# 24 selection steps moved from the prompt to the latent stage, and the prompt's scores in four single banks three heads ahead of their turns

## The chip, the cores and the metric

One core of one Trainium2 chip runs the whole program. The metric is the device time of one execution in microseconds (us); lower is better. Five engines appear: PE (TensorE, the matmul array), DVE (VectorE), ACT (ScalarE), POOL (GpSimd) and SP (SyncE, which issues DMAs). PE reads from SBUF and writes into PSUM, eight banks of 512 f32 columns on each of 128 partitions.

## The reference

The program is one step of a decoder trunk of two layers, on 528 prompt tokens (16 learned ones and 512 given) and on 64 new sample tokens (8 sequences of 8, each with 2048 cached positions). Each layer is a half feed-forward block, an attention block with two groups of eight heads, and another half feed-forward block, each with a layer norm. The two head groups:

```python
# latent heads ("M" in the kernel)
s = (einsum('bqhr,bkr->bhqk', q_lat, c_kv) + einsum('bqhd,bkd->bhqk', q_pe, k_pe)) * scale
p = softmax(where(key_pos <= q_pos, s, -inf)); o_lat = einsum('bhqk,bkr->bqhr', p, c_kv)
# sparse heads ("D"): an indexer picks, for each query, the top_k keys that all 8 heads use
score = einsum('bqh,bqhk->bqk', w_idx, relu(einsum('bqhd,bkd->bqhk', q_idx, k_idx)))
_, sel = lax.top_k(where(key_pos <= q_pos, score, -inf), top_k)   # 132 for prompt, 256 for samples
s = q . k[sel] * 64**-0.5;  o = softmax(s) @ v[sel]
```

The choice of keys is exact: it goes by the order of f32 scores. For the prompt it is needed per query tile, for the samples once per layer, before their sparse heads.

## The kernel before, in words

A loop of two turns (one per layer) runs the stages feed-forward, projection, sample index scores, prompt attention, latent attention of the samples, sparse attention of the samples, output projection, feed-forward, with a barrier between stages. Two stages are touched, and one helper.

**Selection steps.** The 256 best of each sample query's index scores are found in 32 rounds: MAX8 (line L1264) finds the eight best of a row of 1032 values, and MATCH_REPLACE (L1267) strikes them out. That is 63 steps, all on DVE, in turn, and nothing needs them before the sparse sample stage. `sample_step` issues one. 40 of them stand in the prompt stage (after each head in the D passes of tiles 0 to 3 and after eight heads of M passes, by `STEP_UNITS` and `STEP_HEADS`), the other 23 in the latent sample stage, one after each of its slots.

**The prompt stage** (`prompt_block`) goes over 74 units, one per query tile and head. Queries lie in four tiles of 128 rows and a tail of 16 (tile 4, one unit for all heads). The passes come in the order M0, M4, D4, D0, M1, D1, M2, D2, M3, D3; M is latent and D sparse, and tile t has 128(t+1) keys. Each unit goes through a pipeline:

1. PE writes its scores into a PSUM buffer (M: L1503, L1504, and the causal mask L1506; D: L1508 with the chosen keys' bias L1509). In D0, D1 and D2 the same slot first computes one head of the index scores of the next tile (L1484), which POOL weights and sums.
2. DVE reduces the row maximum (`pnmx`, L1677), ACT takes the exponential into `pP` (L1600; a ring of three).
3. One unit later PE transposes `pP` (L1518) and ACT copies the result to `pPT` (L1610).
4. Two units later PE multiplies with the values (L1536; 128 wide in M, 64 in D). After a pass's last head DVE scales (`prinv` L1691, `posb` L1700, called the norm below) out of the same PSUM banks in which the next pass's values go; PE's first values of the next pass wait for `posb`. Then `posb` is transposed (L1555), and for M multiplied once more (L1547).

During the M pass of tile t (1, 2, 3) DVE also picks that tile's keys: 17 rounds of MAX8 (L1649) and MATCH_REPLACE (L1651), three after each of the heads 0 to 4 and two after head 5. The bias follows after head 7 (L1655, L1659), and PE's scores of D's head 0 wait for it (`bias_done`).

Score buffers are two pairs of banks used in turn: each score job waits until the one two before it has been read (`s_read`). The table `plan` holds, for each slot i, what every engine does in it; every engine's instructions are written out in that order, so an instruction that waits holds up all behind it on its engine.

**The latent sample stage** (`sample_block` with M) goes over four pairs of sequences with keys in chunks of 128. Keys are transposed on PE and copied out of PSUM (the k copies, to `MkT`, L2212 on DVE; `who` gives 20 of a pair's 32 to DVE and 12 to ACT), scores are reduced on DVE (L2339), one exponential covers a pair (L2269, ACT), its transposes are copied out (L2199, to `MPT`, half of them on DVE), and the values follow. DVE copies and steps stand in one stream.

Of the kernel before, what the change touches and what calls it, by code (L numbers as in the profile page):

```python
# [1269 lines left out]
def prompt_block(nc, T, S):  # L1270
# [50 lines left out]
    SB = lambda s, r, w: flat[0:r, (s % 2) * 1024:(s % 2) * 1024 + w]  # L1321
# [6 lines left out]
    plan, s_job, b_job = [], 0, 0  # L1328
    b_kind = []
    lag = n + 6  # L1330
    for i in range(lag):
        p = dict(idx=None, dots4=None, sum4=None, s=None, t=[], pv=None, norm=None, ot=[], uv=None)
        if i == 1:
            p["dots4"] = s_job
            s_job += 1
        if i == 3:
            p["sum4"] = s_job
            s_job += 1
        if i < n:
            kind, t, h = units[i]  # L1340
            if kind == "D" and t < 3:
                p["idx"] = (s_job, t + 1, h)
                s_job += 1
            p["s"] = s_job
            s_job += 1
        if 0 <= i - 1 < n:
            for part in range(2 if units[i - 1][1] == 4 else 1):
# [7 lines left out]
        if i - 4 in last and last[i - 4][0] == "M":  # L1355
            p["uv"] = (b_job, last[i - 4][1])
            b_kind.append("X")
            b_job += 1
        if i - 3 in last:
            kind, t = last[i - 3]  # L1360
# [5 lines left out]
    tjob = {i - 1: p["t"][-1] for i, p in enumerate(plan) if p["t"]}  # L1366
# [34 lines left out]
    with nc.Block() as block:  # L1401
# [41 lines left out]
        def _(e):  # L1443
# [15 lines left out]
            for i, p in enumerate(plan):  # L1459
                if p["dots4"] is not None:  # L1460
# [3 lines left out]
                    if s >= 2:  # L1464
                        e.wait_ge(S.s_read, s - 1)
# [5 lines left out]
                if p["sum4"] is not None:  # L1471
                    s = p["sum4"]
                    e.wait_ge(S.s_read, s - 1)
# [4 lines left out]
                if p["idx"]:  # L1478
                    s, t, h = p["idx"]
                    if s >= 2:  # L1480
                        e.wait_ge(S.s_read, s - 1)
# [5 lines left out]
                if p["s"] is not None:  # L1487
# [5 lines left out]
                    if s >= 2:  # L1493
                        e.wait_ge(S.s_read, s - 1)
# [16 lines left out]
                for part, q in enumerate(p["t"]):  # L1511
                    u = i - 1
# [55 lines left out]
        def _(e):  # L1568
# [11 lines left out]
            for i, p in enumerate(plan):  # L1580
# [21 lines left out]
                for part, q in enumerate(p["t"]):  # L1602
                    u = i - 1
# [21 lines left out]
        def _(e):  # L1625
# [45 lines left out]
            for i, p in enumerate(plan):  # L1671
                if i < n:
# [9 lines left out]
                    if (kind, t) in STEP_UNITS or units[i] in STEP_HEADS:  # L1682
                        sample_step(e, T, S, nsround[0])
                        nsround[0] += 1
                if p["norm"]:
# [4 lines left out]
                    e.wait_ge(S.pv_done, i - 1)  # L1690
# [211 lines left out]
def sample_block(nc, T, S, l, kind, cache, new_rows, next_cache=None):  # L1902
# [5 lines left out]
    n = kind  # L1908
# [60 lines left out]
    for q, j in enumerate(order):  # L1969
        who = {"c": "A", "k": "A" if j[1] % 8 in (3, 5, 7) else "D", "p": "A" if j[-1] % 2 else "D", "o": "A" if M else "O"}[j[0]]  # L1970
# [531 lines left out]
```

## Time and profile before

| | us |
|---|---|
| median of 3 runs | 3438.88 (3438.42 to 3440.54) |
| profiled execution, its own time | 3442.29 |
| span of its trace | 3440.6 |
| PE busy | 3012.0 (88%) |
| DVE busy | 1449.1 (42%) |
| ACT busy | 980.9 (29%) |
| POOL busy | 625.1 (18%) |

The busy shares are means over stages with different limits. In layer 0 the prompt stage runs from about 689 to 917 us of the span and the latent sample stage from there to about 1110 us; layer 1 repeats them some 1703 us later. A row that names a line and an engine has the output's and the inputs' names behind it; what stands in brackets at a row's end is the engine's idle time before the instruction, and the instruction that ended it. PEclk (the last column but one) is the share of full speed granted to PE.

### The profile page before, as it was taken

What the parts mean: (1) busy time and instruction counts of PE and PEld (TensorE: products, weight loads), DVE (VectorE), ACT (ScalarE), POOL (GpSimd) and SP (SyncE); (2) the same over time, 40 slices, a digit from 0 to 9 for tenths busy, and PEclk for the clock granted to TensorE, in tenths of its full rate; (3) what the DMA queues carried; (4) which work ended last, traced back from release to release, by engine and by line L of the source; (5) the groups of instructions that cost most, each with busy time, mean ns of one, the idle gap of its engine ahead of it and who ended that gap; (6) DMA issues with size and microseconds to landing.
All of it is one profiled execution on the core that took longest, in us unless ns stands there. A gap on an engine that the chain in (4) does not pass through costs nothing. (4 is left out here: it accounts for less than half of the span.)

```text
span 3440.6 us, 46122 instructions
## 1 busy us (share of the span) xinstructions
PE 3012.0 (88%) x18298; PEld 2581.3 (75%) x18298; DVE 1449.1 (42%) x2150; ACT 980.9 (29%) x1562; POOL 625.1 (18%) x568
## 2 busy tenths in 40 slices
PE   6999979768797879999889999796787978799997
PEld 6999759545565669998689997684555656699985
DVE  2222363478654352222622224534886443422236
ACT  2212233434332221212321223234333322212223
POOL 1111030213122131110311111211121121311103
PEclk9999989879898889999989999898799989899998
DMA  3222441300122322224332234313001223222244
GB/s 109 81 81 88 141 126 51 123 1 1 62 79 77 121 76 79 79 80 134 123 93 79 79 110 141 102 39 123 1 1 62 94 87 116 68 79 80 84 137 129
DMA packets 241754, 293.95 MB, mean 85 GB/s; under 512 B 12624, under 2 KB 205488, under 8 KB 235456
## 3 DMA queue, kind: packets, MB, share of 16 engines
q1 hardware_dynamic: 234688, 229.00, 22.2%
q0 software_dynamic: 6912, 62.92, 5.0%
q8 instruction: 94, 1.54, 0.2%
q14 instruction: 60, 0.49, 0.0%
HBM read 287.72 MB, written 3.88 MB: 85 GB/s over the span
## 5 line engine op out<-in xcount | busy, mean ns | idle before, releaser
L132 DVE TENSOR_TENSOR wlo<-raw,whi 128x1024 fp32r<-128x1024 f32 (+2 forms) x412 | 537.5, 1305 | 1431.3 <-ACT whi L128 1430.1
L128 ACT ACTIVATE whi<-raw 128x1024 fp32r<-128x1024 f32 (+2 forms) x412 | 433.5, 1052 | 1565.3 <-PE ps L467 931.0
L467 PE MATMUL ps<-xth,whi 128*128 128x296 f32 x2816 | 811.4, 300 | 43.3 <-DVE wlo L132 43.3
L467 PE MATMUL ps<-xtl,whi 128*128 128x296 f32 x2816 | 813.7, 301 | 0.0
L467 PE MATMUL ps<-xth,wlo 128*128 128x296 f32 x2816 | 616.1, 301 | 0.0
L467 PEld LDWEIGHTS ps<-xth,whi 128*128 128x128 f32 x2816 | 534.2, 190 | 44.2 <-DVE wlo L132 44.2
L467 PEld LDWEIGHTS ps<-xtl,whi 128*128 128x128 f32 x2816 | 532.8, 189 | 0.0
L467 PEld LDWEIGHTS ps<-xth,wlo 128*128 128x128 f32 x2816 | 461.4, 189 | 0.0
L140 PE MATMUL ps<-whi,hth 128*128 128x512 f32 (+1 forms) x880 | 350.8, 399 | 10.1 <-DVE wlo L132 8.4
L142 PE MATMUL ps<-whi,htl 128*128 128x512 f32 (+1 forms) x880 | 346.9, 394 | 0.0
L141 PE MATMUL ps<-wlo,hth 128*128 128x512 f32 (+1 forms) x880 | 346.8, 394 | 0.0
L446 POOL CAST hth<-hf 128x592 f32 x88 | 59.7, 678 | 990.8 <-DVE hf L417 990.8
L140 PE MATMUL ps<-whi,xth 128*128 128x338 f32 (+1 forms) x480 | 174.8, 364 | 42.2 <-DVE wlo L132 41.9
L140 PEld LDWEIGHTS ps<-whi,hth 128*128 128x128 f32 (+1 forms) x880 | 158.5, 180 | 68.5 <-DVE wlo L132 23.0
L142 PEld LDWEIGHTS ps<-whi,htl 128*128 128x128 f32 (+1 forms) x880 | 158.2, 180 | 45.9
L141 PEld LDWEIGHTS ps<-wlo,hth 128*128 128x128 f32 (+1 forms) x880 | 158.4, 180 | 42.2
L141 PE MATMUL ps<-wlo,xth 128*128 128x338 f32 (+1 forms) x480 | 169.5, 353 | 0.0
L142 PE MATMUL ps<-whi,xtl 128*128 128x338 f32 (+1 forms) x480 | 168.6, 351 | 0.0
L227 POOL TENSOR_SCALAR x<-x,rstd,nb 128x1024 f32<-128x1024 f32 (+2 forms) x30 | 34.8, 1159 | 653.8 <-DVE nb L219 653.8
L1600 ACT ACTIVATE pP<-ps,pnmx 128x256 f32<-128x256 f32 (+4 forms) x132 | 70.4, 533 | 239.2 <-DVE pnmx L1677 239.0
L448 POOL TENSOR_TENSOR htl<-hf,hth 128x592 f32 x88 | 129.1, 1467 | 14.4 <-POOL hth L446 14.4
L140 PEld LDWEIGHTS ps<-whi,xth 128*128 128x128 f32 x480 | 90.8, 189 | 54.4 <-DVE wlo L132 44.9
(379 smaller groups left out, 4036.0 us busy)
## 6 DMA issues: line engine op xcount, KB each, us to landing
raw<-in_ffn_w_in SPq DMA_DIRECT2D x176, 512.0 KB, 3.8
raw<-in_ffn_w_out SPq DMA_DIRECT2D x176, 512.0 KB, 3.5
raw<-in_w_o SPq DMA_DIRECT2D x32, 512.0 KB, 3.6
raw<-in_w_in SPq DMA_DIRECT2D x16, 507.0 KB, 3.8
gb<-in_ln_g SPq DMA_DIRECT2D x6, 512.0 KB, 4.6
gb<-in_ln_b SPq DMA_DIRECT2D x6, 512.0 KB, 5.9
raw<-in_w_in SPq DMA_DIRECT2D x8, 338.0 KB, 3.3
x<-in_x_prompt SPq DMA_DIRECT2D x1, 1536.0 KB, 10.7
```

The source lines that it names most:

```text
L128: e.activation(T.whi[:, s % SPLIT, 0:width], T.raw[:, s, 0:width], ACT.Copy).then_inc(S.hi_done, 1)
L132: e.tensor_tensor(T.wlo[:, s % SPLIT, 0:width], T.raw[:, s, 0:width], T.whi[:, s % SPLIT, 0:width].bitcast(F32), ALU.subtract).then_inc(S. ...
L140: e.matmul(out, lhi, rhi, start=start, stop=False)
L141: e.matmul(out, lhi, rlo, start=False, stop=False)
L142: return e.matmul(out, llo, rhi, start=False, stop=stop)
L227: e.tensor_scalar(x, x, T.rstd[0:r, t:t + 1], T.nb[0:r, t:t + 1], ALU.mult, ALU.add).then_inc(S.norm_done, 1)
L446: e.tensor_copy(h_hi, T.hf[:, u, :]).then_inc(S.hhi_done, 1)
L448: e.tensor_tensor(h_lo, T.hf[:, u, :], h_hi.bitcast(F32), ALU.subtract).then_inc(S.hlo_done, 1)
L467: mm = e.matmul(bank(u, up)[:, h, :], part[:, s, w], xp[:, k, o], start=(k == 0 and part is T.whi and xp is T.xth), stop=(k == KD - 1 and ...
L1600: e.activation(Pb[:, i % 3, 0:NK[t]], SB(p["s"], P, NK[t]), ACT.Exp, bias=nmx[:, i % 3:i % 3 + 1], accum_out=rsum[:, a, c:c + 1]).then_inc ...
```

## The change

Three edits. The numbers of lines behind the change are about 15 higher in the changed kernel.

- 24 of the 40 steps leave the prompt stage: all of D0 and D1 and the eight in M passes. In the latent sample stage two steps stand after each of 24 slots in place of one (47 there in all, the last one single).
- The score buffers are four single banks in place of two pairs, given out by `s_new` (a job of the tail tile takes two). Transposes stand three slots behind their scores, and values and norm four, in place of one and two. The ring of three `pP` buffers stays.
- In the latent sample stage the 20 k copies of a pair that DVE made go to ACT.

```diff
-STEP_UNITS = [("D", 0), ("D", 1), ("D", 2), ("D", 3)]
-STEP_HEADS = [("M", 0, 1), ("M", 0, 2)] + [("M", t, h) for t in (1, 2, 3) for h in (6, 7)]
-STEPS_HERE = 8 * len(STEP_UNITS) + len(STEP_HEADS)
+STEP_UNITS = [("D", 2), ("D", 3)]
+STEPS_HERE = 8 * len(STEP_UNITS)
...
-    SB = lambda s, r, w: flat[0:r, (s % 2) * 1024:(s % 2) * 1024 + w]
+    SB = lambda s, r, w: flat[0:r, s_bank[s] * 512:s_bank[s] * 512 + w]
...
-    lag = n + 6
+    BEHIND = 3
+    plan, b_job = [], 0
+    b_kind, s_bank, s_wait, user = [], [], [], [None] * 4
+    at_bank = 0
+
+    def s_new(banks):
+        nonlocal at_bank
+        if banks == 2:
+            at_bank = (at_bank + 1) // 2 * 2
+        mine = [(at_bank + b) % 4 for b in range(banks)]
+        s_wait.append(max([user[b] for b in mine if user[b] is not None], default=None))
+        s_bank.append(mine[0])
+        for b in mine:
+            user[b] = len(s_bank) - 1
+        at_bank += banks
+        return len(s_bank) - 1
+
+    lag = n + BEHIND + 5
...
             if kind == "D" and t < 3:
-                p["idx"] = (s_job, t + 1, h)
-                s_job += 1
-            p["s"] = s_job
-            s_job += 1
-        if 0 <= i - 1 < n:
-            for part in range(2 if units[i - 1][1] == 4 else 1):
+                p["idx"] = (s_new(1), t + 1, h)
+            p["s"] = s_new(2 if t == 4 else 1)
+        if 0 <= i - BEHIND < n:
+            for part in range(2 if units[i - BEHIND][1] == 4 else 1):
...
-        if 0 <= i - 2 < n:
-            p["pv"] = i - 2
-        if i - 2 in last:
-            p["norm"] = last[i - 2]
+        if 0 <= i - BEHIND - 1 < n:
+            p["pv"] = i - BEHIND - 1
+        if i - BEHIND - 1 in last:
+            p["norm"] = last[i - BEHIND - 1]
...
+    def s_free(e, s):
+        if s_wait[s] is not None:
+            e.wait_ge(S.s_read, s_wait[s] + 1)
...
-                    if s >= 2:
-                        e.wait_ge(S.s_read, s - 1)
+                    s_free(e, s)
                     if kind == "D" and h == 0 and t > 0:
                         e.wait_ge(S.bias_done, chosen.index(t) + 1)
...
-                    if (kind, t) in STEP_UNITS or units[i] in STEP_HEADS:
+                    if (kind, t) in STEP_UNITS:
                         sample_step(e, T, S, nsround[0])
...
-        who = {"c": "A", "k": "A" if j[1] % 8 in (3, 5, 7) else "D", "p": "A" if j[-1] % 2 else "D", "o": "A" if M else "O"}[j[0]]
+        who = {"c": "A", "k": "A" if M or j[1] % 8 in (3, 5, 7) else "D", "p": "A" if j[-1] % 2 else "D", "o": "A" if M else "O"}[j[0]]
...
                     if M and p < PAIRS - 1:
                         step()
+                        step()
```

On PE at the start of the latent pass of tile 3, before: scores are L1503, L1504 and L1506, transposes L1518, values L1536 (128x64 for the sparse pass of tile 2, 128x128 for the latent one), and the transposes of `posb` L1555.

```order
L1536 MATMUL ps<-z,pPT 128x64 x3
L1503 MATMUL ps<-ckvT,qlatT 128x512
L1504 MATMUL ps<-pkeys_4082,combT 128x512
L1506 MATMUL ps<-trib,identb 128x128
L1518 MATMUL ps<-ident,pP 128x128 x4
L1536 MATMUL ps<-z,pPT 128x128 x4
L1555 MATMUL ps<-ident,posb 128x128 x4
L1503 MATMUL ps<-ckvT,qlatT 128x512
L1504 MATMUL ps<-pkeys_4083,combT 128x512
L1506 MATMUL ps<-trib,identb 128x128
L1518 MATMUL ps<-ident,pP 128x128 x4
L1536 MATMUL ps<-z,pPT 128x128 x4
```

And in the changed kernel, where these lines are L1518, L1519, L1521, L1533, L1551 and L1570. The piece begins with the scores of this pass's fourth head; the three before it have the same three rows.

```order
L1518 MATMUL ps<-ckvT,qlatT 128x512
L1519 MATMUL ps<-pkeys_4083,combT 128x512
L1521 MATMUL ps<-trib,identb 128x128
L1533 MATMUL ps<-ident,pP 128x128 x4
L1551 MATMUL ps<-z,pPT 128x64 x3
L1518 MATMUL ps<-ckvT,qlatT 128x512
L1519 MATMUL ps<-pkeys_4082,combT 128x512
L1521 MATMUL ps<-trib,identb 128x128
L1533 MATMUL ps<-ident,pP 128x128 x4
L1551 MATMUL ps<-z,pPT 128x128 x4
L1570 MATMUL ps<-ident,posb 128x128 x4
```

The pass's first values (128x128), which wait for the norm of the sparse pass of tile 2, stood behind the scores of its third head and stand now behind those of its fifth.

DVE in that latent pass, at that norm, in the changed kernel (L1664 and L1666 are the rounds of the key choice, L1706 and L1715 the norm, L1692 the maximum):

```order
L1666 MATCH_REPLACE pwork<-ptop,pwork 128x516
L1664 MAX ptop<-pwork 128x8
L1666 MATCH_REPLACE pwork<-ptop,pwork 128x516
L1706 RECIPROCAL prinv<-prsum 128x8
L1715 TENSOR_TENSOR posb<-ps,prinv 128x512
L1692 TENSOR_REDUCE pnmx<-ps 128x1
L1664 MAX ptop<-pwork 128x8
```

The last rounds ahead of the norm are those of head 3; before, the norm stood behind those of head 1. 

DVE at that pass's end, before: L1264 and L1267 are selection steps, L1655 and L1659 the bias.

```order
L1651 MATCH_REPLACE pwork<-ptop,pwork 128x516
L1677 TENSOR_REDUCE pnmx<-ps 128x1
L1264 MAX slist<-swork 128x8
L1677 TENSOR_REDUCE pnmx<-ps 128x1
L1655 TENSOR_SCALAR pbias<-pwork 128x512
L1659 TENSOR_TENSOR pbias<-pbias,trib 128x128
L1267 MATCH_REPLACE swork<-slist,swork 128x1032
L1677 TENSOR_REDUCE pnmx<-ps 128x1
```

And in the changed kernel, the bias being L1670 and L1674 and steps L1263 and L1266:

```order
L1666 MATCH_REPLACE pwork<-ptop,pwork 128x516
L1692 TENSOR_REDUCE pnmx<-ps 128x1 x2
L1670 TENSOR_SCALAR pbias<-pwork 128x512
L1674 TENSOR_TENSOR pbias<-pbias,trib 128x128
L1692 TENSOR_REDUCE pnmx<-ps 128x1
L1263 MAX slist<-swork 128x8
```

The two steps behind the maxima of heads 6 and 7 are gone.

DVE in the latent sample stage, second pair, before: L2339 are the maxima of the scores, L2212 the k copies, L2199 the copies of the transposed exponentials.

```order
L2339 TENSOR_REDUCE Mst<-ps 128x1 x2
L2347 TENSOR_REDUCE Mst<-Mst 128x1
L2212 CAST MkT<-ps 128x512 x2
L2199 COPY MPT<-ps 128x512
L1264 MAX slist<-swork 128x8
L2212 CAST MkT<-ps 128x512
L2199 COPY MPT<-ps 128x512
L1267 MATCH_REPLACE swork<-slist,swork 128x1032
L2199 COPY MPT<-ps 8x128
```

And in the changed kernel (L2354 the maxima, L2214 the copies of the transposed exponentials):

```order
L2354 TENSOR_REDUCE Mst<-ps 128x1 x2
L2362 TENSOR_REDUCE Mst<-Mst 128x1
L2214 COPY MPT<-ps 128x512
L1263 MAX slist<-swork 128x8
L1266 MATCH_REPLACE swork<-slist,swork 128x1032
L2214 COPY MPT<-ps 128x512
L1263 MAX slist<-swork 128x8
L1266 MATCH_REPLACE swork<-slist,swork 128x1032
L2214 COPY MPT<-ps 8x128
```

The k copies are gone from DVE, and between two copies of exponentials stand two steps.

## Rows read from the trace of the kernel before

**Rows 1.** Busy by stretch: start:end length, PE, PEld, DVE, ACT, POOL, PEclk, DMA.

```profile
730.30:754.40 24.10, 22.80 (x152) 17.38 (x152) 16.27 (x33) 12.93 (x47) 8.90 (x15) 0.83 0.00 1
754.40:778.60 24.20, 16.34 (x89) 12.53 (x88) 22.86 (x70) 7.69 (x26) 0.25 (x2) 0.86 0.00 1
797.50:828.40 30.90, 23.26 (x113) 15.99 (x112) 28.66 (x68) 9.52 (x26) 0.17 (x2) 0.89 0.00 1
852.90:888.70 35.80, 27.19 (x135) 17.61 (x134) 34.20 (x68) 10.62 (x25) 0.00 (x0) 0.90 0.00 1
888.70:917.00 28.30, 23.68 (x165) 17.92 (x163) 18.37 (x26) 13.02 (x29) 0.00 (x0) 0.98 0.00 1
```

**Rows 2.** Waits of PE between 689 and 917 us: total, times, longest.

```profile
PE ps L1518 <- ACT pP L1600: 28.6, 16, 5.4
PE ps L1536 <- DVE posb L1700: 12.1, 6, 4.0
```

**Rows 3.** DVE, order of time: start us, us, operation, [idle before <-releaser].

```profile
702.38 0.29 DVE L1677 TENSOR_REDUCE pnmx<-ps 128x1 f32<-128x128 f32 x1 [0.87 <-PE ps L1506]
...
863.85 0.69 DVE L1700 TENSOR_TENSOR posb<-ps,prinv 128x512 f32<-128x512 f32 x1
...
875.40 0.69 DVE L1677 TENSOR_REDUCE pnmx<-ps 128x1 f32<-128x512 f32 x1
...
884.22 0.69 DVE L1677 TENSOR_REDUCE pnmx<-ps 128x1 f32<-128x512 f32 x1
...
884.83 1.22 DVE L1264 MAX8 slist<-swork 128x8 f32<-128x1032 f32 x1
...
885.97 0.67 DVE L1677 TENSOR_REDUCE pnmx<-ps 128x1 f32<-128x512 f32 x1
```

**Rows 4.** PE in order of time, latent pass of tile 3.

```profile
864.69 2.04 PE L1536 MATMUL ps<-z,pPT 128*128 128x128 f32 x8 [4.04 <-DVE posb L1700]
...
870.81 1.02 PE L1503 MATMUL ps<-ckvT,qlatT 128*128 128x512 f32 x2
...
873.92 1.02 PE L1503 MATMUL ps<-ckvT,qlatT 128*128 128x512 f32 x2
...
887.38 1.10 PE L1508 MATMUL ps<-kT,qaT 128*128 128x512 f32 x2
```

**Rows 5.** Single microseconds, columns as in Rows 1.

```profile
738.00:739.00 1.00, 1.00 (x7) 0.88 (x7) 0.00 (x0) 0.12 (x1) 0.00 (x0) 0.84 0.00 0
...
868.00:869.00 1.00, 1.00 (x4) 0.39 (x3) 0.93 (x4) 0.22 (x1) 0.00 (x0) 0.99 0.00 0
```

**Rows 6.** DVE in order of time, sparse pass of tile 0.

```profile
750.18 0.29 DVE L1677 TENSOR_REDUCE pnmx<-ps 128x1 f32<-128x128 f32 x1
...
751.60 0.29 DVE L1677 TENSOR_REDUCE pnmx<-ps 128x1 f32<-128x128 f32 x1
```

**Rows 7.** PE in order of time, sparse pass of tile 1.

```profile
783.64 0.63 PE L1536 MATMUL ps<-z,pPT 128*128 128x64 f32 x4 [1.04 <-DVE posb L1700]
```

**Rows 8.** End of the prompt stage, in order of time.

```profile
908.78 0.60 PE L1518 MATMUL ps<-ident,pP 128*128 128x128 f32 x4
...
909.22 1.00 PE L1536 MATMUL ps<-z,pPT 128*128 128x64 f32 x8
...
913.06 0.20 DVE L1691 RECIPROCAL prinv<-prsum 128x8 f32<-128x8 f32 x1 [2.19 <-PE ps L1536]
```

**Rows 9.** DVE and ACT in order of time, latent stage of the samples.

```profile
938.48 0.08 DVE L1267 MATCH_VALUE_LOAD swork<-slist,swork 128x8 f32 x1
...
939.79 1.24 DVE L1264 MAX8 slist<-swork 128x8 f32<-128x1032 f32 x1
...
952.51 0.69 DVE L2199 COPY MPT<-ps 128x512 f32<-128x512 f32 x1 [1.45 <-PE ps L2103]
...
978.38 1.11 ACT L2269 ACTIVATE MP<-ps,Mst 128x1024 f32<-128x1024 f32 x1
...
1008.04 1.11 ACT L2269 ACTIVATE MP<-ps,Mst 128x1024 f32<-128x1024 f32 x1
```

More of the change, by code:

```diff
@@ L1333, in prompt_block @@
         if i == 1:
-            p["dots4"] = s_job
-            s_job += 1
+            p["dots4"] = s_new(2)
         if i == 3:
-            p["sum4"] = s_job
-            s_job += 1
+            p["sum4"] = s_new(2)
         if i < n:
@@ L1350, in prompt_block @@
                 b_job += 1
-        if 0 <= i - 2 < n:
-            p["pv"] = i - 2
-        if i - 2 in last:
-            p["norm"] = last[i - 2]
-        if i - 4 in last and last[i - 4][0] == "M":
-            p["uv"] = (b_job, last[i - 4][1])
+        if 0 <= i - BEHIND - 1 < n:
+            p["pv"] = i - BEHIND - 1
+        if i - BEHIND - 1 in last:
+            p["norm"] = last[i - BEHIND - 1]
+        if i - BEHIND - 3 in last and last[i - BEHIND - 3][0] == "M":
+            p["uv"] = (b_job, last[i - BEHIND - 3][1])
             b_kind.append("X")
             b_job += 1
-        if i - 3 in last:
-            kind, t = last[i - 3]
+        if i - BEHIND - 2 in last:
+            kind, t = last[i - BEHIND - 2]
             for a in range(2 if kind == "M" and t < 4 else 1):
@@ L1365, in prompt_block @@
         plan.append(p)
-    tjob = {i - 1: p["t"][-1] for i, p in enumerate(plan) if p["t"]}
+    def s_free(e, s):
+        if s_wait[s] is not None:
+            e.wait_ge(S.s_read, s_wait[s] + 1)
+    tjob = {i - BEHIND: p["t"][-1] for i, p in enumerate(plan) if p["t"]}
     ot_job = {(kind, t): q for p in plan for q, kind, t, a in p["ot"]}
@@ L1472, in _ @@
                     s = p["sum4"]
-                    e.wait_ge(S.s_read, s - 1)
+                    s_free(e, s)
+                    e.wait_ge(S.s_read, plan[1]["dots4"] + 1)
                     e.wait_ge(S.wsel_set, 1)
@@ L1479, in _ @@
                     s, t, h = p["idx"]
-                    if s >= 2:
-                        e.wait_ge(S.s_read, s - 1)
+                    s_free(e, s)
                     r = QT[t]
@@ L1492, in _ @@
                         e.wait_ge(S.pe_keys, 4)
-                    if s >= 2:
-                        e.wait_ge(S.s_read, s - 1)
+                    s_free(e, s)
                     if kind == "D" and h == 0 and t > 0:
@@ L1511, in _ @@
                 for part, q in enumerate(p["t"]):
-                    u = i - 1
+                    u = i - BEHIND
                     kind, t, h = units[u]
@@ L1602, in _ @@
                 for part, q in enumerate(p["t"]):
-                    u = i - 1
+                    u = i - BEHIND
                     kind, t, h = units[u]
```

6 lines of the change are left out of this document (1 added, 5 removed).

## The prediction

> **What bounds the kernel now.** I read the busy time by stretch first, then the waits of PE, then DVE and PE in order of time around each place that the change touches, all in layer 0; layer 1 has the same form, so every sum is doubled at the end. The page says 88% PE, but the two touched stages differ. In the latent passes of tiles 1, 2 and 3 DVE is the one that is nearly full: 22.86 of 24.20 us, 28.66 of 30.90, 34.20 of 35.80, with PE at 16.34, 23.26 and 27.19 and its clock at 0.86 to 0.90 [rows 1]. In the sparse passes it is PE: 22.80 of 24.10 us around D0, where DVE has 16.27 [rows 1]. So PE's largest waits in the stage, 28.6 us on ACT's exponentials and 12.1 us on `posb` [rows 2], lie mostly in latent passes, where they cost nothing: PE waits because DVE paces the pass. That is what the deeper lookahead removes, and so it can give only what is waited for elsewhere.
>
> **The change part by part, per layer.** Steps in latent passes: in M3 the step after head 6 lies between two maxima on DVE, 884.83 to 885.97, 1.14 us [rows 3]. The one after head 7 stands behind the bias and hides in the time until D3's scores and their maximum. So on DVE alone D1, D2 and D3 could start 1.1 us earlier each. What is late next is PE. In the changed order the first values of a latent pass wait for a norm that DVE reaches only after the rounds of head 3. In M3 the maximum of head 4 started 11.55 us after `posb` (863.85 to 875.40), and that stretch holds `posb` itself (0.6) and one more copy (0.6), which come later now; `posb` is thus written from 863.85 + 11.55 - 1.2 = 874.2 to 874.9. PE waited 4.04 us at this place and resumed at 864.69 [rows 4]; now it resumes at 874.9 after about 8 us. From there to the maximum of head 7, which releases the bias, it owes three heads' worth of scores, transposes and values: 3 x 3.11 = 9.33 us at the full clock, a head being 870.81 to 873.92 [rows 4]. A wait of 4.04 us was followed by work at clock 0.50 until about 868.0, 3.3 us after it resumed; in 868 to 869 it read 0.99 [rows 5]. Work at half the clock loses half its length, 1.65 us; I bound it by 3.0. So the maximum of head 7 starts at 885.9 to 887.2, where before it started at 885.97 [rows 3]: D3 starts 0 to 1.2 us later, I take +0.4. In M1 and M2 the keys are fewer: PE's three heads shrink to about 16.34/27.19 and 23.26/27.19 of 9.33 (5.6 and 8.0, upper ends, as these sums hold stretches at half clock), DVE's remaining rounds, some 9.9 us in M3 (from 874.9 to 884.8), only to 6.6 and 8.3 [rows 1]. With the slow stretch PE is late by 0.65 and somewhat under 1.35 against a start that is 1.14 earlier: M1 -0.3, M2 -0.2. The ends for each of the three are -1.1 (PE never late) and +1.3.
>
> M0: DVE waited 0.87 us for PE before one maximum [rows 3]; two slots of transposes and values now come after it. -0.4, between -0.9 and 0. The two steps there (M0) lie beside DVE's waits and give nothing more.
>
> D0: the pass is one of PE's. 24.10 - 22.80 = 1.3 us is idle, and part of it is at clock 0.50, as 738 to 739 shows PE full at 0.84 just after it has risen [rows 1, 5]. Heads come every 1.42 us [rows 6], with DVE's eight steps beside them. Steps gone and the lookahead there, I take the idle 1.3; the ends are 0 and -2.2 (POOL's weighting, 8.90 us in this stretch, sets a pace near that of PE). The lookahead here is smaller than the name says: a head of D0 to D2 takes two of four banks, so its scores wait for the exponential two heads back.
>
> D1: PE waits 1.04 us for `posb` [rows 7], since DVE had steps ahead of the norm; those are gone and the values stand two slots later. -1.0 (0 to -1.1). D2 and D3 keep their steps and are full of PE: 23.68 of 28.30 us with the drain [rows 1]. 0 (-0.5 to +0.3).
>
> The drain is where the lookahead is paid back. Before, 4.28 us passed from the last scores (908.78) to the norm (913.06), with one set of transposes (908.78 to 909.22, 0.44) and two of values in them [rows 8]. Now four sets of transposes, 1.76 us, and five of values stand behind the last scores; a set of values is the rest of that row's 1.00 us less the overlap, 0.84, so 4.2 us: about 6.0 against 4.28. +1.8, between +1.4 and +2.2.
>
> Prompt stage: -0.4 - 1.3 - 1.0 - 0.3 - 0.2 + 0.4 + 1.8 = **-1.0**.
>
> Latent sample stage: 24 more steps at 1.31 us a match (938.48 to 939.79) and 1.27 a maximum (1.24 and its gap) [rows 9] are 31 us on DVE. The 20 k copies a pair that leave DVE, 0.6 us each, are 12 of 29.66 us, the distance between two exponentials (978.38 to 1008.04) [rows 9]. In the first pair the added steps fall into time in which DVE waits for keys: no loss. ACT gets one k copy ahead of the first exponential: +0.45. In the second and third pair DVE's stream between two exponentials is then 3.6 (to the first copy of transposed exponentials) + 8 x 2.58 (two steps) + 4.3 (maxima, copies, norm) + 1.5 (a wait of 1.45 for PE, as before that copy now [rows 9]) = 30.0 to 30.2, against 29.66. DVE and PE are close to level, so the second pair gives some +0.75, the third +0.5 and the fourth, which has no steps, nothing: **+1.8**, with ends +0.5 and +3.0. ACT takes 0.6 x 20 = 12 us more in a pair and stays under 29.66. The SP queue's key swap waits for the last step but has the sparse stage's first half ahead of it: 0.
>
> The sum is +0.8 per layer, +1.6 for two. The profiled execution took 3442.29, which gives 3443.9; it lay 3.4 above the median of its three runs, 3438.88, so the number that compares is **3440.5 us**.
>
> The rule that speaks against the prompt part: the Trainium skill, "TensorE: Matmul & The Clock Gate", section "HAM oscillation — how this bites in real kernels", tells of a kernel whose TensorE was kept fed already, in which further PSUM double-buffering gained nothing. By it the prompt part would be 0 instead of -1.0, and the sum +3.6, 3442.5 us, inside the range and inside "same". This trace agrees for M1 to M3 and not for D1, where PE does wait 1.04 us [rows 7].
>
> **The rivals.** First, the latent passes stay DVE's. If PE catches up in time after the late norm, D1, D2 and D3 start 1.1 us earlier each, -3.3 in place of -0.1 together; if the sample stage then costs only its lower end, +0.5 in place of +1.8, a layer comes to 0.8 - 3.2 - 1.3 = -3.7, and the whole to 3438.9 - 7.4 = **3431.5 us**. For it: 28.66 to 34.20 us of DVE against 23.26 to 27.19 of PE [rows 1], so PE has 5 to 7 us in hand over a pass. Against: the late norm puts that slack ahead of the last three heads, where it is lost. Chance 0.25.
>
> Second, the slower side: the slow clock after the wait for `posb`. PE idles twice as long as at 864.69, and comes back at 0.50. Around D0, where PE is busy nearly throughout, the mean clock of 0.83 over 24.10 us is 0.17 x 24.10 / 0.5 = 8.2 us at half speed [rows 1], up to about 738 [rows 5]. If it lasts so long in each of M1 to M3, PE loses 4 us where the middle of my bounds is 2.3, and the bias is late by some 1.6 us more in each pass: 3 x 1.6 = 4.9 with the rounding, so +5.7 a layer, 3438.9 + 11.4 = **3450.3 us**. It decides once the stretch at 0.50 is longer than 6 us. For it: that stretch around D0. Against: the 3.3 us in M3 [rows 4, 5]. Chance 0.20.
>
> Third, DVE's stream in the latent sample stage becomes the bound in full: a copy of transposed exponentials waits behind two steps where it waited behind one, 1.29 us more; for three sets of values in pairs 2 and 3 that is +3.9 more per layer, **3448 us**. Chance 0.09.
>
> Fourth, the change doesn't do what it says: with three `pP` buffers, two banks a head and the same engine orders, the lookahead changes nothing in D0 to D2, and only the drain and the latent stage remain, offset by the steps that left. That gives 3439 to 3443, chance 0.08.
>
> **How the numbers follow.** This leaves 0.38 for the forecast. Within 0.2% (about what a measurement of this kernel can tell from no change) is 3432.0 to 3445.8. Forecast and fourth case fall inside it, 0.46 in all; the first gives faster, with a little of it inside, which the forecast's own lower tail makes up for: 0.24; the second and third are slower, with the forecast's upper tail: 0.30. The forecast's own range, from the bounds of its terms, is 3434 to 3447. The range that leaves out no more than 2 in 10 reaches to both first rivals: 3430 to 3451.
>
> **What would show it.** Right: in M3 a wait of PE for `posb` near 8 us with clock 0.50 behind it; DVE idle before the maximum of head 7; no wait for `posb` in D1; about 6 us from the last scores to the last norm; 30 us between exponentials of the samples against 29.66. Wrong: DVE above 34 of 35 us in M3 with D3 starting earlier (first rival); a stretch at 0.50 longer than 6 us (second); copies of transposed exponentials with long idle PE before the values (third). The whole is wrong if a stage that the diff does not touch moves by more than a few us.

## The result and the profile after

The changed kernel takes 3445.98 us (median of 19 runs, 3441.32 to 3456.03), the kernel before 3439.46 us (19 runs, 3435.90 to 3446.23). The ratio is 1.0019, 95% interval 1.0013 to 1.0026: 6.5 us slower, inside the range forecast (3430 to 3451) and 5.5 us above the number forecast. Its profiled execution took 3445.35 us. One of the eleven executions of the kernel normfirst, in the table of experiments, took 4844.65 us at a mean granted clock of 0.578 in place of 0.93, and its ratio leaves that one out. The head of the changed kernel's page:

```profile
span 3443.3 us, 46122 instructions
PE 3012.4 (87%) x18298; PEld 2583.5 (75%) x18298; DVE 1428.4 (41%) x2110; ACT 1000.0 (29%) x1602; POOL 625.0 (18%) x568
```

PE's work is the same; some 20 us of DVE's went to ACT (1449.1 to 1428.4 and 980.9 to 1000.0). Where the time went is read from starts of passes, not from shares. The table's second column is the start in the span of the kernel before. The other two are the changed kernel minus the kernel before, both counted from the start of the prompt stage, from the traces of one execution each (a second one of the changed kernel is under the experiments):

| start of | layer 0, before | layer 0, changed | layer 1, changed |
|---|---|---|---|
| D0 | 735.74 | -1.24 | -1.29 |
| M1 | 753.11 | -0.98 | -1.07 |
| D1 | 777.66 | -0.78 | -0.88 |
| M2 | 795.90 | -2.11 | -2.21 |
| D2 | 827.43 | -2.70 | -2.80 |
| M3 | 850.83 | -2.71 | -2.81 |
| D3 | 887.38 | -1.13 | -1.16 |
| last norm | 913.30 | +1.48 | +1.45 |
| 1st exponential of the latent sample stage | 948.97 | +1.45 | +1.12 |
| 2nd | 978.38 | +1.92 | +1.59 |
| 3rd | 1008.04 | +2.41 | +2.08 |
| 4th | 1037.64 | +2.42 | +2.09 |

So 2.7 us are won up to M3 and more than lost in M3 (+1.6) and in D3 with its drain (+2.6). The drain is the time from the last scores to the last norm. The stretches that answer to [rows 1], in the changed kernel, same columns (three numbers follow POOL's: PE's clock, the DMA share and GB/s, so the clock is the third from the end and not the last but one):

```profile
730.20:753.40 23.20, 22.28 (x150) 17.58 (x151) 7.04 (x20) 12.87 (x47) 8.45 (x15) 0.82 0.01 1
753.40:778.10 24.70, 18.36 (x87) 14.25 (x86) 21.14 (x66) 7.47 (x26) 0.81 (x3) 0.72 0.01 1
795.80:825.90 30.10, 23.29 (x104) 15.75 (x104) 26.07 (x66) 9.29 (x26) 0.23 (x2) 0.83 0.00 1
850.20:887.10 36.90, 27.98 (x128) 17.53 (x126) 32.06 (x65) 10.39 (x25) 0.00 (x0) 0.81 0.00 0
887.10:917.00 29.90, 27.11 (x191) 20.86 (x189) 17.67 (x25) 13.88 (x31) 0.00 (x0) 0.98 0.01 2
```

DVE is no longer nearly full in M3 (32.06 of 36.90 us against 34.20 of 35.80), and the clock fell from 0.86, 0.89 and 0.90 to 0.72, 0.83 and 0.81. The waits of PE, which answer to [rows 2], and the one of D1 that was 1.04 us [rows 7]:

```profile
PE ps L1551 <- ACT pPT L1625: 24.6, 11, 5.5
PE ps L1551 <- DVE posb L1715: 13.2, 6, 5.1
```

```profile
785.61 0.63 PE L1551 MATMUL ps<-z,pPT 128*128 128x64 f32 x4 [0.24 <-DVE posb L1715]
```

The first two add up to 37.8 us against 40.7: the lookahead did not remove PE's waits, it moved them from transposes to values. What waits in M3, on PE and on DVE in order of time:

```profile
857.81 0.88 PE L1551 MATMUL ps<-z,pPT 128*128 128x64 f32 x6 [1.65 <-ACT pPT L1625]
...
862.98 0.88 PE L1551 MATMUL ps<-z,pPT 128*128 128x64 f32 x6 [2.02 <-ACT pPT L1625]
...
872.46 2.05 PE L1551 MATMUL ps<-z,pPT 128*128 128x128 f32 x8 [5.12 <-DVE posb L1715]
```

```profile
871.62 0.69 DVE L1715 TENSOR_TENSOR posb<-ps,prinv 128x512 f32<-128x512 f32 x1
...
884.97 0.69 DVE L1692 TENSOR_REDUCE pnmx<-ps 128x1 f32<-128x512 f32 x1 [1.88 <-PE ps L1521]
```

And PE's clock there, same columns:

```profile
866.00:867.00 1.00, 1.00 (x6) 0.76 (x4) 0.97 (x3) 0.06 (x1) 0.00 (x0) 0.50 0.00 0
...
877.00:878.00 1.00, 1.00 (x3) 0.35 (x2) 0.97 (x2) 0.00 (x0) 0.00 (x0) 0.50 0.00 0
878.00:879.00 1.00, 1.00 (x7) 0.51 (x6) 0.33 (x2) 0.00 (x0) 0.00 (x0) 0.79 0.00 0
```

The clock is already at 0.50 while PE still works (866 to 867), stays there through the wait of 5.12 us, and for 6 us of work behind it. In layer 1 it fell some 3.5 us later, inside the wait, and rose at the same place of the pass; M3 is as long there (38.20 us against 38.13), so it is the stretch behind `posb` that costs. DVE, which before was waited for, now waits 1.88 us for PE ahead of head 7's maximum. The bias stands behind that maximum, and D3's scores wait for the bias.

The drain of D3, on PE and on DVE in order of time, answers to [rows 8]:

```profile
907.79 0.60 PE L1533 MATMUL ps<-ident,pP 128*128 128x128 f32 x4
908.22 1.00 PE L1551 MATMUL ps<-z,pPT 128*128 128x64 f32 x8
...
910.03 1.10 PE L1551 MATMUL ps<-z,pPT 128*128 128x64 f32 x8 [0.36 <-ACT pPT L1625]
...
914.69 0.20 DVE L1706 RECIPROCAL prinv<-prsum 128x8 f32<-128x8 f32 x1 [4.81 <-PE ps L1551]
```

From the transposes behind the last scores to the norm it takes 6.90 us, where it was 4.28. The same piece in the kernel before, of which [rows 8] shows the beginning and the end, went on like this:

```profile
910.54 0.66 PE L1518 MATMUL ps<-ident,pP 128*128 128x128 f32 x4 [0.32 <-ACT pP L1600]
911.03 1.99 PE L1536 MATMUL ps<-z,pPT 128*128 128x64 f32 x16
```

In the latent sample stage the distance between the second and third exponential is 30.15 us against 29.66 [rows 9]. ACT in order of time, and behind it the stretch between these two exponentials with the columns of [rows 1]:

```profile
979.97 0.59 ACT L2225 ACTIVATE MkT<-ps 128x512 fp32r<-128x512 f32 x1
980.45 1.12 ACT L2284 ACTIVATE MP<-ps,Mst 128x1024 f32<-128x1024 f32 x1
```

```profile
980.45:1010.60 30.15, 28.93 (x184) 20.70 (x182) 23.51 (x34) 14.23 (x27) 6.65 (x4) 1.00 0.28 93
```

A k copy stands right in front of the exponential, and it costs 0.48 us of start to start. PE is busy for 28.93 of the 30.15 us and DVE for 23.51, so DVE, with all its steps, is not what paces the pair.

### The profile page after: what moved, and what is told of

Read it like the earlier page. It is cut to its first block and busy times, and to the rows that moved or that the text cites. A ratio compares the mean times of both kernels' runs of the same rounds, so it can differ in the third digit from the quotient of the medians.

```text
span 3443.3 us, 46122 instructions
## 1 busy us (share of the span) xinstructions
PE 3012.4 (87%) x18298; PEld 2583.5 (75%) x18298; DVE 1428.4 (41%) x2110; ACT 1000.0 (29%) x1602; POOL 625.0 (18%) x568
## 3 DMA queue, kind: packets, MB, share of 16 engines
q8 instruction: 92, 1.51, 0.2%
## 5 line engine op out<-in xcount | busy, mean ns | idle before, releaser
L1551 PE MATMUL ps<-z,pPT 128*128 128x128 f32 (+1 forms) x672 | 106.4, 293 | 78.9 <-ACT pPT L1625 50.1
L1551 PEld LDWEIGHTS ps<-z,pPT 128*128 128x128 f32 x672 | 93.6, 207 | 89.8 <-ACT pPT L1625 57.4
```

Source lines behind the costliest of these rows:

```text
L1551: mm = e.matmul(flat[:, o:o + w], PT[0:kr, u % 2, k * P:(k + 1) * P], v, start=k == kts[0][0], stop=k == kts[-1][0])
```

## The experiments

My theory after the result: the longer lookahead is what costs (late norm, half clock, drain), while the moved steps give about 1 us in each latent pass. Rival: the moved steps and the k copies cost. Each kernel's name stands in brackets at its experiment. Each ratio is to the kernel before, run on the same chip (its median there 3438.5 to 3440.2 us), with its 95% interval; "prompt" is the shift of the last norm against the start of its stage, in layer 0 and layer 1.

| kernel | median us | ratio | prompt |
|---|---|---|---|
| changed | 3445.98 | 1.0019 (1.0013 to 1.0026) | +1.48, +1.45 |
| steps | 3441.50 | 1.0010 (1.0001 to 1.0019) | -1.09, -1.51 |
| look | 3449.44 | 1.0031 (1.0019 to 1.0043) | +1.16, +2.18 |
| normfirst | 3445.44 | 1.0016 (1.0006 to 1.0025) | -0.79, +4.52 |
| heads8 | 3455.92 | 1.0048 (1.0034 to 1.0061) | -0.38, -1.25 |
| behind1 | 3438.94 | 1.0002 (0.9993 to 1.0011) | -3.25, -1.86 |
| kact | 3444.94 | 1.0021 (1.0012 to 1.0030) | +0.33, +0.13 |
| kdve | 3466.42 | 1.0089 (1.0070 to 1.0107) | +0.08, +1.28 |
| warmafter | 3437.90 | 1.0001 (0.9992 to 1.0009) | -2.97, -3.19 |
| warm0 | 3431.34 | 0.9973 (0.9963 to 0.9983) | -1.82, -2.19 |
| best | 3432.10 | 0.9979 (0.9970 to 0.9988) | -3.01, -3.54 |

**Steps and k copies alone** (steps), the changed kernel with the old lookahead and with two banks for each score job, as before:

```diff
-    BEHIND = 3
+    BEHIND = 1
     def s_new(banks):
+        banks = 2
```

> The score buffers and the lookahead of before (two pairs of banks, transposes one slot and values two behind); the steps and the k copies as in the changed kernel. Theory (the lookahead is what costs: late norm, half clock, longer drain): the prompt stage ends about 4 us earlier per layer than before (1.1 us each in M1, M2, M3 for the step after head 6, about 1 in D1), the latent sample stage takes +1.0 as in the changed kernel; about -3 us per layer, -6 in all, ratio near 0.998. Rival (the moved steps and the k copies are what costs): the prompt stage within 1 us of before, the whole 2 to 6 us slower, ratio 1.001 to 1.002.

The prompt stage won 1.1 and 1.5 us, not 4; the latent stage took +0.6 and +0.2. The whole is 0.1% slower, with an interval that just leaves out no change. The time is the rival's at its lower end, and the trace has neither's numbers. Start to start, D1 is 1.05 us shorter in both layers and M2 0.6, M3 0.2 longer, and D0 and M1 stay: the steps cost D1 1 us, where DVE had them ahead of the norm, and nothing like 1 us in each latent pass.

**The lookahead alone** (look): the step tables, the single step a slot and the k copies of before in the changed kernel.

> Only the single banks and the lookahead of three; steps and k copies as before. Theory: the drain +2.6 us, and in M1 to M3 the steps after head 6 stand again beside a PE that comes late from the wait for posb: D2 and D3 start 1 to 2 us later than before, the prompt stage +2 to +4 us per layer, the latent stage 0; +4 to +8 in all. Rival (the lookahead is neutral or a gain, the steps cost): the prompt stage -1 to +1 us, the whole within 3 us of before.

The lookahead (with its single banks) costs in the prompt stage about what the changed kernel has there, +1.2 and +2.2, and the latent stage is nearly untouched (+0.40 and +0.03). The drain is +2.6 as in the theory, but it is the only place: D2 and D3 start 1.9 and 1.5 us earlier than before in layer 0, 1.0 and 0.4 in layer 1, where the theory had them 1 to 2 us later. M3 is 0.44 and 0.54 us longer, with a wait of 6.34 us for `posb` and then 3.6 and 3.8 us at clock 0.50. So the prompt stage lies under the theory's +2 to +4 in layer 0 and inside it in layer 1, and the time above its +4 to +8 (+10.7 us by the ratio).

**The eight steps of latent passes alone** (heads8):

```diff
-STEP_HEADS = [("M", 0, 1), ("M", 0, 2)] + [("M", t, h) for t in (1, 2, 3) for h in (6, 7)]
+STEP_HEADS = []
...
                         step()
+                    if M and p == 0:
+                        step()
```

> The kernel before with the eight steps in latent passes of the prompt alone moved, to the first pair of the latent sample stage (two steps a slot there), where DVE waits for keys. Theory: M1, M2, M3 each 1.1 us shorter, nothing lost in the latent stage; -3 us per layer, -6 in all, ratio near 0.998. Rival (PE's work paces the passes, or the first pair has no room): under 1 us per layer either way.

Both halves of the theory fell. The passes M1, M2 and M3, which lost the steps, changed by +0.23, 0.00 and +0.67 us in layer 0 and +0.22, +0.01 and +0.56 in layer 1 (start to start). DVE in M3 there, at the maximum behind `posb` and at the end:

```profile
871.13 0.69 DVE L1677 TENSOR_REDUCE pnmx<-ps 128x1 f32<-128x512 f32 x1 [0.71 <-PE ps L1506]
...
885.13 0.69 DVE L1677 TENSOR_REDUCE pnmx<-ps 128x1 f32<-128x512 f32 x1
886.50 0.69 DVE L1677 TENSOR_REDUCE pnmx<-ps 128x1 f32<-128x512 f32 x1 [0.67 <-PE ps L1506]
```

Without the step between them the last two maxima are 1.37 us apart, with it 1.75 [rows 3]: of the step's 1.14 us only 0.38 came off, since head 7's scores stand on PE behind the transposes that wait for head 5's exponential. Most of the step had filled a wait. That M3 is longer is not the edit's doing: the kernels warm0 and best below have M3 as before, with its steps, and it takes 0.6 to 0.8 us more there too. In all three the clock stays at 0.50 for 5.7 to 6.1 us after PE resumes behind `posb`, where it was 3.3 and 3.5 us before, and DVE waits for PE at the next maximum. And the first exponential of the latent stage came 7.9 us (7.2 in layer 1) later than the prompt's end explains. There PE waits for DVE's k copies, which stand behind two steps:

```profile
941.90 0.66 PE L2058 MATMUL ps<-ident,Mks 128*128 128x128 f32 x4 [1.21 <-DVE MkT L2212]
...
947.57 0.65 PE L2058 MATMUL ps<-ident,Mks 128*128 128x128 f32 x4 [1.52 <-DVE MkT L2212]
```

and on DVE each copy and each maximum behind a pair of steps, here a copy and the first maximum:

```profile
944.35 1.24 DVE L1264 MAX8 slist<-swork 128x8 f32<-128x1032 f32 x1
945.62 0.09 DVE L1267 MATCH_VALUE_LOAD swork<-slist,swork 128x8 f32 x1
945.70 1.22 DVE L1267 MATCH_REPLACE8 swork<-slist,swork 128x1032 f32<-128x1032 f32 x1
946.84 0.68 DVE L2212 CAST MkT<-ps 128x512 fp32r<-128x512 f32 x1
...
949.91 0.68 DVE L2339 TENSOR_REDUCE Mst<-ps 128x1 f32<-128x512 f32 x1
```

The prediction had this stretch as time in which DVE waits for keys. It does wait there, but each piece of the wait ends when a key arrives, and a step in it delays that key's copy.

**The k copies.** On ACT alone, in the kernel before (kact):

```diff
-"k": "A" if j[1] % 8 in (3, 5, 7) else "D"
+"k": "A" if M or j[1] % 8 in (3, 5, 7) else "D"
```

> The kernel before with the k copies of the latent sample stage on ACT alone. The kernel with eight moved steps lost 7.5 us up to the first exponential of that stage, the changed one lost none. Theory (k copies waiting on DVE behind steps delay PE's keys; ACT has no such queue): the first exponential comes 2 to 3 us earlier than before, the other three distances between exponentials stay within 0.3 us of 29.6; -4 to -6 in all. Rival (ACT's copies are on the path themselves): first exponential later by 0 to 1 us.

The rival holds: the first exponential +0.54 and +0.17 against the last norm, then +0.47 and +0.49 for the next two distances and 0 for the last. The changed kernel has the same three distances, and this kernel has none of its moved steps. The first exponential has no such match: in the changed kernel it is 0.03 and 0.33 us earlier against the last norm. ACT in front of the second exponential:

```profile
980.80 0.59 ACT L2210 ACTIVATE MkT<-ps 128x512 fp32r<-128x512 f32 x1
981.28 1.12 ACT L2269 ACTIVATE MP<-ps,Mst 128x1024 f32<-128x1024 f32 x1
```

So in the trace the 24 steps themselves are free there, once the copies are gone from DVE. The time does not agree: 1.0021 is 7 us, as much as the whole change, where the trace has 3.1 for both layers. The reverse edit in the changed kernel (kdve):

> The changed kernel with the 20 k copies of a pair back on DVE, two steps a slot kept. Theory (a k copy that waits on DVE behind two steps delays PE's keys; that is what the move to ACT prevents): the first exponential 7 us later than in the changed kernel, the distances between the next ones 1 to 3 us longer; +8 to +12 us per layer, the whole 3460 to 3470. Rival (the steps fit beside the copies, ACT's copies are the only cost): 1.5 us per layer less than the changed kernel.

Near what was expected: counted from the last norm, the first exponential is 8.2 and 7.3 us later than in the changed kernel, the next distance 3.4 and 3.7 us longer (above the 1 to 3 expected) and the one after it 0.8, 12.4 and 11.7 us a layer in all. So in the traces the move of the k copies costs 1.5 and 1.1 us a layer (kact) and is what makes room for the steps.

**Lookahead of one with single banks** (behind1: `BEHIND = 1` in the changed kernel, nothing else):

> The changed kernel with the single banks kept and the lookahead back at one slot (transposes one behind, values two). Theory (the lookahead is the cost, the banks are neutral): the prompt stage as in the kernel with the old buffers and moved steps, 1.1 us shorter per layer than before and 2 to 3 shorter than the changed one, the clock mean at 0.931 to 0.932; the whole near 3441. Rival (the four single banks cost something of their own): more than 1 us per layer beside the kernel with old buffers, the whole 3444 or more.

The banks are no cost: D0 took 1.8 and 1.3 us less than before, where in "steps" it took +0.01 and -0.1. The ratio is 0.0017 below the changed kernel's, and the prompt stage is 4.7 and 3.3 us shorter than its. Counted from M1's start, which leaves out the spread up to there (see the second traces), it is 3.5 and 3.1 us. M3 gives 1.2 and 1.1 of them and D3 with its drain 2.7, and the passes before M3 take 0.4 and 0.7 back: this is the lookahead's price.

**The norm ahead of the rounds** (normfirst), on DVE in each slot:

```diff
+                if p["norm"]: ...
                 if i < n: choose(...); sample_step(...)
-                if p["norm"]: ...
```

> The changed kernel with one edit: on DVE a slot's norm (reciprocal and posb) stands ahead of that slot's three rounds of the key choice. posb in M3 comes about 4.6 us earlier. Theory (PE's late start after posb and the half clock behind it make D3 late): PE's wait of 5.1 us for posb in M3 nearly goes, M3 is 1 to 2.5 us shorter than in the changed kernel, M2 and M1 0.3 to 1.5, the drain unchanged; 1.5 to 4 us per layer less than the changed kernel, so the whole between 3438 and 3443. Rival (D3 is late for another reason, as the single banks or the exponentials' ring): posb earlier, D3's start unchanged, the whole near 3446.

M3 took -0.13 us against before in layer 0 and +1.31 in layer 1, where the changed kernel has +1.58 and +1.65: for layer 0 the late norm is behind the loss, layer 1 doesn't show it. There the clock was low again at the end of M3 and once more in D3 (0.83 in 2580 to 2590 and in 2600 to 2610). Part of what was won in layer 0, and more than that in layer 1, went again in D3, where the wide norm of M3 now stands ahead of that slot's step and the next maximum, and PE waits through ACT:

```profile
892.71 1.22 DVE L1708 TENSOR_TENSOR posb<-ps,prinv 128x1024 f32<-128x1024 f32 x1
```

```profile
897.18 0.63 PE L1570 MATMUL ps<-ident,posb 128*128 128x128 f32 x4 [1.58 <-ACT pPT L1625]
```

From D3's start to the last norm it takes 3.3 and 5.0 us more than before, against 2.6 in the changed kernel, and the time is the changed kernel's within the interval.

**PE kept busy** (warmafter), before the values of each of twelve latent slots, 37 a layer:

```diff
+                more = FILL.get(units[i] if i < n else None, 0)
+                if more:
+                    s = plan[i + 1]["s"]
+                    s_free(e, s)
+                    for _ in range(more):
+                        e.matmul(SB(s, P, 512), T.ident[:, :], T.ckvT[:, 0:512], start=True, stop=True)
```

> The changed kernel with 37 extra matmuls (128x512, f32, thrown away: they write the bank of the next slot's scores before those do) in the latent passes, placed where PE waits, so that it stays busy. Theory (the half clock after the late norm is what makes D1 to D3 start late): the clock reads near 1.00 through M1 to M3 and in D0, the 6 us at 0.50 behind posb in M3 go, D3 starts 2 to 3 us earlier than in the changed kernel, D0's heads at its start are 3 to 4 us faster; 5 to 8 us per layer less, the whole between 3430 and 3438. Rival (the clock is incidental, the order of the norm alone counts): starts of D1 to D3 within 0.7 us of the changed kernel, the whole near 3445.

M3 in it (window, then PE in order of time; L1543 are the extra matmuls):

```profile
848.00:885.00 37.00, 34.57 (x156) 19.92 (x156) 33.27 (x67) 11.44 (x28) 0.00 (x0) 1.00 0.00 0
```

```profile
863.13 5.32 PE L1543 MATMUL ps<-ckvT,ident 128*128 128x512 f32 x12
869.63 0.57 PE L1560 MATMUL ps<-z,pPT 128*128 128x128 f32 x3 [1.18 <-DVE posb L1724]
...
881.84 1.02 PE L1526 MATMUL ps<-kT,qaT 128*128 128x512 f32 x2
```

With the clock at 1.00, M3 took 0.14 us less than before in place of 1.58 more, with the norm as late as in the changed kernel (869.40 to 881.84 is 12.4 us to D3's start; in the changed kernel 872.3 to 886.4, 14.1). D3 starts 4.4 and 4.6 us earlier than in the changed kernel, of which 1.4 are there at D0's start. So M3's loss is the half clock's, and the late norm matters through it. The other traces say the same. For both layers, how far into M3 PE resumes behind `posb`, how long the clock stays at 0.50 from there, and how much longer M3 is than before, in us:

| kernels | resume | at 0.50 behind it | M3 |
|---|---|---|---|
| before, kact | 13.9 | 3.3 to 3.5 | 0.0 |
| steps | 13.9 | 5.2 | +0.2 |
| behind1 | 13.9 | 5.4, 5.7 | +0.35, +0.5 |
| heads8, warm0, best | 13.9 | 5.7 to 6.1 | +0.6 to +0.8 |
| look | 24.2 | 3.6 to 3.9 | +0.4 to +0.6 |
| changed, kdve | 24.2 | 5.7 to 6.1 | +1.5 to +1.65 |

M1 and M2 are the changed kernel's to 0.3 us, though there the clock had fallen to 0.72 and 0.83: in these passes the half clock cost little. The drain is unchanged (+2.5). The whole is in the range expected (3430 to 3438), and the gain is smaller than the 5 to 8 us a layer: 3.5 in the trace, 6 for both layers by the ratios.

**The same where it is on PE's path in the kernel before** (warm0): 17 extra matmuls ahead of the transposes in M0's heads 5 to 7 and M4.

> The kernel before with 17 such matmuls in M0 and M4 alone, before the transposes there. Theory (8 us at half clock around D0 lie on PE's path): D0 ends 3 to 4 us earlier per layer, all later stages keep it; -6 to -8 us in all, ratio 0.998. Rival (they get in the way, or the clock stays at 0.50 all the same): 0 or later.

PE from 733 to 741 us, first before, then in this kernel:

```profile
733.00:741.00 8.00, 8.00 (x47) 7.24 (x48) 3.95 (x7) 4.11 (x12) 0.48 (x1) 0.67 0.00 0
```

```profile
733.00:741.00 8.00, 7.70 (x65) 6.62 (x67) 5.49 (x11) 4.76 (x15) 1.69 (x3) 1.00 0.00 0
```

M1 starts 2.7 and 3.2 us earlier, and the whole is 0.27% faster than the kernel before, the fastest that was run. The theory had all later stages keep what was won, and they keep two thirds of it: M3 takes 0.7 and 0.8 us more than before, since DVE waits for PE behind `posb` as in heads8, and at the last norm 1.8 and 2.2 us are left.

```profile
869.19 0.69 DVE L1685 TENSOR_REDUCE pnmx<-ps 128x1 f32<-128x512 f32 x1 [0.59 <-PE ps L1509]
```

With single banks beside it (best):

> The kernel before (its steps, its k copies, its lookahead of one) with the four single banks and the 17 extra matmuls in M0 and M4. The single banks alone, with the moved steps beside them, made D0 about 1.5 us shorter than the old pairs did; the extra matmuls took 2 to 3 us per layer. Theory (both are on PE's path and add up): D1 starts 4 us or more earlier per layer than before; the whole 3426 to 3431, ratio 0.996 to 0.9975. Rival (at full clock D0 is held by POOL or by DVE's steps, and the banks give nothing): as with the extra matmuls alone, 3429 to 3433, D0's start to M1's start no shorter than there.

The theory's number is missed: D1 starts 3.3 and 3.6 us earlier, not 4. M1 starts 3.61 and 3.99 us earlier, 0.9 and 0.8 more than in warm0, but D0 itself is no shorter than there (-0.8 in both layers against before, -0.8 and -1.1 in warm0), as in the rival, and the time shows no gain (0.9979 beside 0.9973; the intervals overlap). Whether the banks are worth something is open.

**Second traces.** The changed kernel again (after2) and the lookahead again (look2):

> The changed kernel once more, for a second trace: tells how far one trace's stages vary. Theory (M passes and drain are the same each time, transfers vary): starts of D0 to D3 against the stage's start within 0.5 us of the first trace, the drain within 0.1; the stages around it differ by up to 3 us.

> The kernel with the lookahead alone once more. Its profiled execution (3437.5) was the lowest of six and 11 us under their median, at a mean clock of 0.932 against 0.926 to 0.928 in the others. Theory (the half clock in the latent passes did not come every time): a lower mean clock than in the first trace and D2 or D3 starting 1 us or more later against the stage's start, where PE waited for posb. Rival: the prompt stage as in the first trace within 0.5 us, and the other 10 us in stages that the edit does not touch.

Of the changed kernel's second trace the pass starts lie within 0.36 us of the first's (last norm +1.82, +1.10) and D3 with its drain within 0.03 us, while its time was 3448.72; the first exponential of layer 0 came 2.1 us later. Of look's second trace the passes lie within 0.5 us of the first, though its mean clock was 0.928, and the time is 3445.25 in place of 3437.45. That is the rival's case: nearly all of these 8 us lie in stages that the edit does not touch. A wider spread shows up to D0. The prompt stage of kdve is the changed kernel's to the letter, and in layer 0 its D0 starts 2.46 us earlier than before, where the changed kernel's two traces have 1.24 and 1.06; from the start of M0 to that of D0 its mean clock was 0.63 against 0.58. From D0 on its passes are the changed kernel's within 0.2 us. So one trace of a kernel tells the cost of a pass behind D0 to 0.2 us, the start of D0 to no better than 1.4, and the time of the program to no better than some 8. So the traced stages sum to +4.5 us for the changed kernel (2.42 + 2.09), the timed runs give +6.5 (4.5 to 8.9), and the 2 us between are within that. For look, steps, kact and warm0 time and traced sum differ by 4 to 7 us, both ways, and that was not explained.

## Why the prediction was right, point by point

The time is inside the range and the sign is the one forecast, but the parts are less right than the whole, and part of that is luck. The prompt stage was to win 1.0 us and lost 1.5; the latent sample stage was to lose 1.8 and lost 0.8. The two errors have opposite signs, and 2.5 us of the one are offset by 1.0 of the other.

- **M0, forecast -0.4; measured -0.39 and -0.45** up to M4's start. D0's start is earlier by another 0.85 us, since transposes and values that stood between D4 and D0 stand behind D0's first scores now; that work is only moved.
- **D0, forecast -1.3; measured +0.26 and +0.22**, or -0.6 with the 0.85 us just named. The term failed in part. Behind1, with a lookahead of one, has D0 1.8 and 1.3 us shorter, at an unchanged start in layer 1: the idle time could be removed, by the single banks and not by the steps (the kernel steps has 0.0 and -0.1) nor by the lookahead. At M1's start the changed kernel has -1.0 and -1.1 (kdve, with the same prompt stage, -2.3 and -1.3) and behind1 -2.2 and -1.3: up to there the traces resolve no gain of the lookahead and no loss. M0, M4, D4 and D0 together took 1.0 us less where 1.7 was forecast for M0 and D0.
- **D1, forecast -1.0; measured -1.33 and -1.33.** Right: the wait of 1.04 [rows 7] is 0.24 now. Steps alone gives 1.05 of it.
- **M1 and M2, forecast -0.3 and -0.2; measured +0.20 and -0.59** (+0.19 and -0.59 in layer 1). Inside the bounds given.
- **M3, forecast +0.4 with bounds of -1.1 and +1.3; measured +1.58 and +1.65.** The mechanism was right in its parts: `posb` 23 us into the pass, PE resumes at 0.50, DVE waits ahead of head 7. Two sizes were off. PE's wait for `posb` was 5.12 us (6.33 in layer 1) and not near 8, with waits of 1.65 and 2.02 us for ACT before it. That cost nothing, for the resume came where it was forecast, counted from the pass's start. Mis-sized was the slow stretch behind it: 6 us of work at 0.50, a loss of 3.0, the upper bound. "Work at half the clock loses half its length, 1.65 us" took the length from the kernel before, where 3.3 us of work were slow. In look 3.6 and 3.8 us were slow, and M3 lost 0.44 and 0.54, which is the term as forecast. The second rival's condition ("once the stretch at 0.50 is longer than 6 us") was just reached in M3, and warmafter puts its price at 1.7 us there (1.58 against -0.14), but M1 and M2 did not pay it.
- **"On DVE alone D1, D2 and D3 could start 1.1 us earlier each" was wrong.** Heads8 shows no earlier start; the step after head 6 stood beside PE's own chain. With it falls the first rival, whose time of 3431.5 needed that gain.
- **The rule cited** from the Trainium skill, "TensorE: Matmul & The Clock Gate", section "HAM oscillation — how this bites in real kernels", is that PSUM double-buffering gave no further gain in a kernel whose loop had been rebuilt so that TensorE's clock stays up. By it the prompt part was to be 0; measured was +1.5, and not the -1.0 of the sum. That is no test of it: in behind1 more score buffers alone did shorten D0 (1.8 and 1.3 us), where the clock was low at first (0.93 in the mean of D0 in the kernel before). In best, with the clock at 1.00 in D0, they did not, and there the traces agree with the page.
- **The drain, forecast +1.8; D3 with drain measured +2.6.** Outside the bounds of 1.4 to 2.2. The reading of [rows 8] was wrong: the 4.28 us held two sets of transposes and three of values (908.78, 909.22, 910.54 and 911.03, the last with two sets) and a wait of 0.32 us for ACT, not one set and two. So the changed kernel has two sets of each more. By the prediction's own prices that is 2 x 0.44 + 2 x 0.84 = 2.6 us, what was measured. The four and five sets forecast for the changed kernel are right.
- **The latent sample stage, forecast +1.8; measured +0.94 and +0.64.** The k copy in front of an exponential was the right mechanism at the wrong place: it costs nothing before the first (-0.03 and -0.33) and 0.5 us before each of the second and third. DVE's chain of 30.0 to 30.2 us hit the distance (30.15) by luck: kact has the same distance without the moved steps, and in the changed kernel DVE is idle for 6.6 us of it. One count was wrong: the description of the kernel and the prediction have 20 k copies on DVE and 12 on ACT in a pair, and the trace has these numbers in a whole stage, four to six on DVE for a pair. So about 3 us a pair went from DVE to ACT and not 12. Nothing in the sum hung on that number.

Sum per layer: forecast +0.8, traced +2.4 and +2.1. The sign and the size class held, the parts partly for the wrong reasons.

## What to carry to other kernels

A deeper lookahead also delays what stands at a pass's end: ask on which engine the norm stands, behind what, and what clock the matmul engine comes back with. A gain read from one engine's busy share is a gain only if the next instruction on it isn't waiting already for another engine; take the filler out alone and look. A few thrown-away matmuls in a wait that precedes a PE-bound stretch are worth more here (0.27% of the time; 3.7 us of it are in the traced stages) than all rearrangement of steps and buffers. And count what a stretch holds in the full order of instructions before pricing what is added to it.

## What the runs showed of the hardware

- In M3 of the changed kernel the clock fell to 0.50 at about 865 in layer 0, before the long wait, after two waits of 1.65 and 2.02 us; it rose at about 878.4, after 6 us of work. In layer 1 it fell some 3.5 us later, inside the wait. In the kernel before it fell at about 861.2, inside a wait, and rose 3.3 us after the resume; in warm0, whose M3 is the same, it rose 5.8 and 6.1 us after it, and M3 was 0.7 and 0.8 us longer.
- 37 extra matmuls a layer (six of them took 5.32 us) raised the mean clock of the whole program from 0.927 to 0.944, and the ratio to the kernel before went from 1.0019 to 1.0001, which is 6 us.
- Two executions of one kernel (look and look2) differ by 7.8 us, of which 0.7 lie in the traced stages.
